# Head norms on token lanes and a band mask added by TensorE, in a two-block transformer kernel

## The reference, cut to what matters

```
def rms_norm_2(x, g):                      # over the 64 of one head
    y = xf * rsqrt(mean(xf * xf, axis=-1) + EPS)
    return y * g

# kind C: keys of the tokens (masked to |q - k| <= 128), context keys, and a sink
s_loc = where(abs(qpos - kpos) <= 128, (q @ k.T) * 64 ** -0.5, -inf)
s_ctx = (q @ k_ctx.T) * 64 ** -0.5
p = softmax(concat([s_loc, s_ctx, sink]))

# kind D
yd = global_attention(apply_rope(rms_norm_2(d_q, qn_g)), apply_rope(rms_norm_2(d_k, kn_g)), d_v,
                      rms_norm_2(cd_k, kn_g), cd_v)
```

## Time and profile before

| what | value |
|---|---|
| median of 3 runs | 2424.68 us (2417.89 to 2424.94) |
| the profiled execution's own time | 2422.05 us |
| its span in the trace | 2420.2 us |
| PE busy | 2194.9 us (91%) |
| DVE, ACT, POOL busy | 752.2, 634.4, 739.4 us |
| layer 0's mixer | from about 1040 to 1223 us of the span |
| layer 1's mixer | from about 1782 to 1920 us of the span |

### The profile page before, as it was taken

One profiled execution on the slowest core, in us unless ns is written; L12 is line 12 of the kernel. 1 busy time (PEld: TensorE's weight loads), 2 busy tenths in 40 slices (PEclk: granted clock), 3 DMA queues, 4 the chain that ended last, 5 costly groups with the idle time before them and its releaser, 6 DMA issues.

```text
span 2420.2 us, 32871 instructions
## 1 busy us (share of the span) xinstructions
PE 2194.9 (91%) x13382; PEld 1354.8 (56%) x13382; DVE 752.2 (31%) x1440; ACT 634.4 (26%) x925; POOL 739.4 (31%) x624
## 2 busy tenths in 40 slices
PE   7998999999799999999999999999889996888886
PEld 7876789878687898865543333333257642222221
DVE  4864220122622212377523222222147420010101
ACT  3544333434544334212512000010022420000001
POOL 7665367897283777710300000000000200000000
PEclk9999999999899999999999999999999998999997
DMA  9433759755157697441215899999962369999997
GB/s 299 140 118 126 261 199 317 244 179 178 36 182 254 208 324 241 143 177 39 86 53 209 341 427 429 429 429 428 424 232 78 134 277 423 427 428 429 429 428 307
DMA packets 151381, 635.98 MB, mean 263 GB/s; under 512 B 7816, under 2 KB 14216, under 8 KB 120920
## 3 DMA queue, kind: packets, MB, share of 16 engines
q1 hardware_dynamic: 148224, 623.78, 66.4%
q0 software_dynamic: 2608, 9.25, 1.3%
q10 hardware_dynamic: 424, 1.22, 0.2%
HBM read 633.17 MB, written 1.05 MB: 262 GB/s over the span
## 4 chain that ended last, share of the span: by engine, by line
PE 65%; DMA 20%; DVE 7%; ACT 3%; POOL 3%; issue 2%; SPq 1%; DVEq 0%; ACTq 0%; POOLq 0%
PE bank L1375 14%; PE bank L624 9%; PE bank L626 9%; PE bank L625 9%; DMA ring<-in_w_gate 9%; DMA ring<-in_w_up 8%; PE bank L1188 4%; PE bank L1333 3%; DMA ring<-in_w_down 3%; PE bank L847 2%; PE bank L1197 2%; PE bank L970 2%; POOL ring_r L1639 2%; PE bank L824 1%; PE bank L1205 1%
## 5 line engine op out<-in xcount | busy, mean ns | idle before, releaser
L1375 PE MATMUL bank<-ring,arena 128*32 128x512 f32 x4424 | 657.4, 630 | 120.6 <-DMA ring<-in_w_gate 53.9
L1639 POOL TENSOR_TENSOR ring_r<-ring,ring_r 128x512 fp32r<-128x512 f32 (+1 forms) x468 | 575.2, 1274 | 294.4 <-ACT ring_r L1734 265.6
L1375 PEld LDWEIGHTS bank<-ring,arena 128*32 128x32 f32 x4424 | 192.7, 115 | 560.3 <-issue 536.6
L624 PE MATMUL bank<-ring_r 128*128 128x256 f32 (+1 forms) x1504 | 463.4, 308 | 14.2 <-POOL ring_r L1639 8.6
L626 PE MATMUL bank<-xT_r,ring_r 128*128 128x256 f32 x1248 | 354.9, 284 | 0.0
L625 PE MATMUL bank<-ring_r 128*128 128x256 f32 x1104 | 312.9, 283 | 0.0
L624 PEld LDWEIGHTS bank<-ring_r 128*128 128x128 f32 x1504 | 289.8, 193 | 37.4 <-issue 18.0
L1734 ACT ACTIVATE ring_r<-ring 128x2048 fp32r<-128x2048 f32 (+1 forms) x119 | 216.7, 1827 | 289.2 <-DMA ring<-in_ffn_w_gu 141.2
L626 PEld LDWEIGHTS bank<-xT_r,ring_r 128*128 128x128 f32 x1248 | 240.1, 192 | 0.0
L625 PEld LDWEIGHTS bank<-ring_r 128*128 128x128 f32 x1104 | 211.6, 192 | 0.7 <-issue 0.5
L1668 POOL TENSOR_TENSOR arena<-const 128x1024 f32<-128x1024 f32 x6 | 12.0, 2003 | 594.8 <-DVEq L2288 525.5
(11 more groups left out here) (356 smaller groups left out, 2720.3 us busy)
## 6 DMA issues: line engine op xcount, KB each, us to landing
ring<-in_w_gate SPq DMA_DIRECT2D x52, 2048.0 KB, 17.2
ring<-in_w_up SPq DMA_DIRECT2D x52, 2048.0 KB, 17.3
ring<-in_w_down SPq DMA_DIRECT2D x40, 2048.0 KB, 18.1
ring<-in_ada_w SPq DMA_DIRECT2D x41, 1024.0 KB, 7.5
ring<-in_w_down SPq DMA_DIRECT2D x41, 1024.0 KB, 18.2
ring<-in_ffn_w_gu SPq DMA_DIRECT2D x35, 1024.0 KB, 5.6
ring<-in_w_up SPq DMA_DIRECT2D x18, 1024.0 KB, 8.7
ring<-in_w_gate SPq DMA_DIRECT2D x17, 1024.0 KB, 5.0
```

Source lines behind the costliest of these rows:

```text
L624: pe.matmul(dst, w_hi, v_hi, start=first, stop=False)
L1375: mm = pe.matmul(dst[nb][CAP * b:CAP * b + CAP, :], src[:, c, CAP * b:CAP * b + CAP], rooms[b % G], start=bi_first, stop=bi_last)
L1639: pool.tensor_tensor(lo[:, c], whole[:, c], hi_of(u)[:, c, 0:n], ALU.subtract).then_inc(*signal("w_lo", (u, c)))
```

## The change

The squares' sums of kind D come out with tokens on the partitions: per tile of 128 tokens the squares are the stationary operand and two columns of `blk64` (one for each head) move, so that a chunk's sums are 128x8 (128x4 for layer 1's queries). Mean, root and reciprocal run on these. Then `spread_norms` brings the inverses back: for each tile and head one product has the token lane's inverse, repeated 64 times by a stride of 0, as the stationary operand and the identity as the moving one, and writes 64 partitions of 128 columns. DVE multiplies with this from the bank. `dq0`, `dq1` are spread between `square_sums2` of `dk0` and the rotations of `cq0`, `cq1`; `dk0` after chunk `ab0`. The banks are 6, 7 and 5; banks 6 and 7 are also those of the rotations of `cq0` and `cq1`.

The band mask becomes a product of the identity with the mask's 256 columns, added to the first key block's scores in the bank, between the products of key block 0 and 1. A masked unit then takes DVE's and ACT's path of a unit without one.

```diff
-        qvar = area(1024, 2, 2 * SEQ)
+        qvar = area(1024, 3, 2 * 4)
@@ unit, block2_units
-  keys=256 * len(tok), size=1024, bias=con("winmask")...
+  keys=256 * len(tok), size=1024, mask=con("winmask")...
@@
+        NORM_AT = dict(dq0=0, dq1=1, dk0=2)
+        SPREAD_BANK = dict(dq0=6, dq1=7, dk0=5)
@@ scores (PE)
                             for c in range(nk):
+                                masked = u["mask"] is not None and kb == 0
                                 mm = pe.matmul(b[:, at:at + 256], u["q"][c][:, t * P:t * P + P], u["k"][kb][c],
-                                               start=(c == 0), stop=(c == nk - 1))
+                                               start=(c == 0), stop=(c == nk - 1 and not masked))
+                            if masked:
+                                mm = pe.matmul(b[:, at:at + 256], ident, u["mask"][:, t, :], start=False, stop=True)
@@ square_sums2 (PE)
-                        pe.matmul(b[:, 0:n], con("blk64"), sq[:, i, 0:n], start=True, stop=True).then_inc(...)
+                        for t in range(n // P):
+                            mm = pe.matmul(b[:, 2 * t:2 * t + 2], sq[:, i, P * t:P * t + P], con("blk64")[:, ::HD], start=True, stop=True)
+                        mm.then_inc(*filled_now(("qss", layer, name)))
+                def spread_norms(names):
+                    for name in names:
+                        n = n_tok if name[1] == "q" else 2 * SEQ
+                        pe.wait_ge(*after("ssq", ("root", layer, name)))
+                        b = open_bank(("rn", layer, name), SPREAD_BANK[name])
+                        for t in range(n // P):
+                            for h in range(2):
+                                one_head = qvar[:, NORM_AT[name], 2 * t + h:2 * t + h + 1].to_broadcast([P, HD])
+                                mm = pe.matmul(b[HD * h:HD * h + HD, P * t:P * t + P], one_head, ident, start=True, stop=True)
+                        mm.then_inc(*filled_now(("rn", layer, name)))
@@ order (PE)
                             square_sums2(("dk0",))
+                            spread_norms(("dq0", "dq1"))
                             rotations(("cq0", "cq1"))
@@
                         chunk("ab0", wb, 0)
+                        spread_norms(("dk0",))
                         rotations(("ck0", "dq0", "dq1"))
@@ roots (ACT)
+                        v = qvar[:, NORM_AT[name], 0:2 * (n_tok if name[1] == "q" else 2 * SEQ) // P]
-                        act.activation(qvar[:, i, 0:n], qvar[:, i, 0:n], ACT.Sqrt).then_inc(...)
+                        act.activation(v, v, ACT.Sqrt).then_inc(...)
@@ norms (DVE), n = 2 * tokens / 128 in the sums and reciprocals
+                    for name in names:
+                        dve.wait_ge(*after("rstd", ("qk", layer, name)))
+                        link(dve.reciprocal(r, r))
+                        done("ssq", ("root", layer, name))
+                    for name in names:
+                        dve.wait_ge(*full(("rn", layer, name)))
-                        link(dve.scalar_tensor_tensor(v, v, col(...), qvar[:, i, 0:n], ALU.mult, ALU.mult))
+                        link(dve.scalar_tensor_tensor(v, v, col(...), bank_of(key)[:, 0:n], ALU.mult, ALU.mult))
+                        drop(key)
```

More of the change, by code:

```diff
@@ L503, in build, with unit @@
         block = ctx.enter_context(nc.Block())
-        def unit(stage, i, q, k, scale, v, y, keys=256, bias=None, sink_at=None, size=512, parts=None):
-            return dict(deep=4 if size == 1024 and i not in (2, 3) else 2, key=(stage, i), n=i, q=q, k=k, scale=scale, v=v, y=y, keys=keys, bias=bias, sink=sink_at, size=size, parts=parts)
+        def unit(stage, i, q, k, scale, v, y, keys=256, bias=None, sink_at=None, size=512, parts=None, mask=None):
+            return dict(deep=4 if size == 1024 and i not in (2, 3) else 2, key=(stage, i), n=i, q=q, k=k, scale=scale, v=v, y=y, keys=keys, bias=bias, sink=sink_at, size=size, parts=parts, mask=mask)
         def half(t, c, j, n0=0, n=SEQ):
@@ L547, in block2_units @@
                                        [(y_hi[64 * (h % 2):64 * (h % 2) + 64, 2 * kind + h // 2, SEQ * s:SEQ * s + SEQ], 64 * (h % 2))],
-                                       keys=256 * len(tok), size=1024, bias=con("winmask").rearrange("p (t k) -> p t k", t=2)
+                                       keys=256 * len(tok), size=1024, mask=con("winmask").rearrange("p (t k) -> p t k", t=2)
                                        if (kind, s) == (0, 0) else None, sink_at=sink[:, layer, h:h + 1] if kind == 0 else None))
@@ L1215, in square_sums2 @@
                         b = open_bank(("qss", layer, name), 4 + i)
-                        pe.matmul(b[:, 0:n], con("blk64"), sq[:, i, 0:n], start=True, stop=True).then_inc(*filled_now(("qss", layer, name)))
+                        for t in range(n // P):
[11 more added lines that the diff above has]
+                        mm.then_inc(*filled_now(("rn", layer, name)))
                 def rotations(names):
@@ L2152, in roots @@
                     for name in names:
-                        n, i = n_tok if name[1] == "q" else 2 * SEQ, int(name[2])
+                        v = qvar[:, NORM_AT[name], 0:2 * (n_tok if name[1] == "q" else 2 * SEQ) // P]
                         act.wait_ge(*after("ssq", ("qk", layer, name)))
-                        act.activation(qvar[:, i, 0:n], qvar[:, i, 0:n], ACT.Sqrt).then_inc(*signal("rstd", ("qk", layer, name)))
+                        act.activation(v, v, ACT.Sqrt).then_inc(*signal("rstd", ("qk", layer, name)))
                 if layer:
@@ L2794, in _ @@
                 for names, others in ((("dq0", "dq1"), ("cq0", "cq1")), (("dk0",), ("ck0",))):
-                    for i, name in enumerate(names):
-                        n = n_tok if name[1] == "q" else 2 * SEQ
+                    for name in names:
+                        n = 2 * (n_tok if name[1] == "q" else 2 * SEQ) // P
                         key = ("qss", layer, name)
                         dve.wait_ge(*full(key))
-                        link(dve.tensor_scalar(qvar[:, i, 0:n], bank_of(key)[:, 0:n], 1.0 / HD, EPS, ALU.mult, ALU.add))
+                        link(dve.tensor_scalar(qvar[:, NORM_AT[name], 0:n], bank_of(key)[:, 0:n], 1.0 / HD, EPS, ALU.mult, ALU.add))
                         drop(key)
                         done("ssq", ("qk", layer, name))
-                    for i, name in enumerate(names):
+                    for name in names:
+                        r = qvar[:, NORM_AT[name], 0:2 * (n_tok if name[1] == "q" else 2 * SEQ) // P]
+                        dve.wait_ge(*after("rstd", ("qk", layer, name)))
+                        link(dve.reciprocal(r, r))
+                        done("ssq", ("root", layer, name))
+                    for name in names:
                         n = n_tok if name[1] == "q" else 2 * SEQ
-                        dve.wait_ge(*after("rstd", ("qk", layer, name)))
-                        link(dve.reciprocal(qvar[:, i, 0:n], qvar[:, i, 0:n]))
+                        key = ("rn", layer, name)
+                        dve.wait_ge(*full(key))
                         v = qk[:, QK_AT[name], 0:n]
-                        link(dve.scalar_tensor_tensor(v, v, col("qn" if name[1] == "q" else "kn", layer), qvar[:, i, 0:n], ALU.mult, ALU.mult))
+                        link(dve.scalar_tensor_tensor(v, v, col("qn" if name[1] == "q" else "kn", layer), bank_of(key)[:, 0:n], ALU.mult, ALU.mult))
+                        drop(key)
                         done("rms", ("qk", layer, name))
```

## The result

The changed kernel took 2429.61 us (median; 2427.39 to 2434.65 over the seven executions compared) against 2420.07 for the kernel before in the same comparison (eight executions, 2414.82 to 2424.94): ratio 1.0037, 95% interval 1.0024 to 1.0051. One further execution of the changed kernel, 2544.08 us at a mean clock of 0.866, is a slow one and stands outside these numbers. So the change costs about 9.5 us, 0.4%. The profiled execution of the changed kernel took 2427.39 us, with a span of 2425.6.

The account below looks back on a forecast made before the run. PE was taken to set layer 0's pace, while in layer 1 it waits for DVE and ACT. Layer 0's +10.7 us (spreads, mask products, shape changes, new wait) and layer 1's 0 gave 2434 us, range 2424 to 2440.

Parts of the forecast that it names:

- What decides: Layer 0 up to `ah1`: PE alone sets the pace, so added PE work is paid in full, DVE relief worth nothing.
- Squares' sums: PE's sums of squares in the norms: 0 of change, bounds -0.1 and +0.1 us for each of six chunks.
- Mean, root, reciprocal: Norms on 128x8: 0.3 us each, hidden behind PE in layer 0, shortening the chain before `dk0`'s rotation in layer 1.
- Spreads: PE products bringing inverses back: 3.4 us in layer 0, 2.2 in layer 1, plus 0.7 us of shape changes per layer.
- the alternating halves of the earlier trace: Lower bound for one spread instruction on PE: the two halves run beside each other, 0.055 us at 128 columns.
- The full-width row: Upper bound for one spread instruction on PE: a full-width product with 128 moving columns, 0.114 us.
- The new wait: PE waits for DVE's multiplication before the rotation of `cq1`: 0.4 us in layer 0, bounds 0.2 and 1.0.
- Mask products and shape changes: PE's masked units, each layer: 3.4 us for the products, 3.0 us for changes of the array's shape around them.
- the +4.7 of the rival: Free shape changes in an unbroken PE group: 3.0 us less in each layer, +4.7 us, 2428; chance 23%.
- Layer 1: Second mixer: 2.4 us gained up to the scores, 2.3 lost from there to `ah1`; +0.1 gained, taken as 0.
- To the end: Output projection and experts after both mixers: both layers' differences pass to the end in full, net +10.7 us.
- the rival at 6%: Layer 0's experts absorb its 10.7 us delay, leaving layer 1's gain: -2 us, 2422; chance 6%.

Follow-up runs that it names:

- e2: Only the band mask's half of the change, norms as in the kernel before: 2429.29 us against 2422.99 for the kernel before, ratio 1.0024.
- e8: The changed kernel with spreads ordered as all tiles of head 0, then head 1: 2428.73 us against 2424.48 for the kernel before, one execution.
- e3: The changed kernel with the mask's products put into the banks before the scores: 2422.56 us against 2422.99 for the kernel before, ratio 0.9987.
- e7: The kernel of e4 run again: 2424.41 us against 2424.48 for the kernel before, ratio 0.9996.
- e4: The whole change in layer 1 alone, layer 0 as in the kernel before: 2430.80 us against 2422.99 for the kernel before, ratio 1.0022.

## Why the prediction was right

**What decides.** Right: in layer 0 every added instruction was paid, and the relief of DVE was worth nothing (e2: all of 6.13 us). Of the 10.5 us that the stages lost, 10.2 stand ahead of layer 0's `ah1`.

**Squares' sums.** Taken at 0: 16 instructions from 1098.10 to 1099.91 are 1.81 us, the four of before 1.82 (1098.56 - 1096.74); `dk0`'s eight take 0.88 (1114.88 - 1114.00) against 0.86. So 0 is right. With 2 moving columns one instruction takes 0.113 us (1.81 / 16), as much as one with 128.

**Mean, root, reciprocal.** Taken at 0.3 us each. The mean at 1120.96 and the end of the reciprocal at 1121.75 in layer 0 give 0.8 us for the three, hidden as said.

**Spreads.** Taken at 0.07 us an instruction plus 0.36 us for each pair of shape changes. One instruction took 0.054 us (see e8), 2.6 us for 48, where 3.4 were predicted: exactly the bound that the alternating halves of the earlier trace rows had given. The tile's shape set the pace, the loading of weights added nothing to be seen, and I should have taken that bound. The full-width row was far off. The Trainium skill, "TensorE: Matmul & The Clock Gate", Part 3, has a load overlap a running product only where their row groups differ; by the prediction's estimate from it the loads would have added about 2.5 us in layer 0, and the trace disagrees, since the 48 took 2.6 us in all.

**The new wait.** 0.4 us predicted in front of the rotation of `cq1`; the row shows 0.32. But that isn't all it costs: there are 0.12 us more in front of the rotation of `cq0`, and the two rotations take 1.50 us (1118.48 - 1116.98) where they took 0.87 (1114.30 - 1113.43): behind a wait the two instructions of one rotation start 0.29 us apart instead of 0.22, and the next group starts later too. That makes 0.75 us, inside the bounds of 0.2 to 1.0. All of the norms' half in layer 0 is 4.05 against 4.5; 2.6 and 0.75 taken off, 0.7 are left for the changes of shape, as predicted. So two terms were mis-sized against each other, the spreads by 0.8 us too much and the wait by 0.35 too little, and it is luck that the sum came out within 0.5.

**Mask products and shape changes.** 3.4 + 3.0 us predicted, less 0.2 for the wait in front of `ah0`, so 6.2; 6.13 measured in layer 0's stage, of which e3 gives 3.04 to the changes. Two units' scores took 6.94 us, forecast 6.7 to 7.1. This term made the difference between "slower" and "no change to be told": without it the sum would have been the +4.7 of the rival.

**Layer 1.** Gain of 2.4 us to the scores predicted, 2.20 measured; PE's wait there 1.0 predicted, 1.09 measured; from there to `ah1` 2.3 lost predicted, 2.55 measured. Net +0.1 gained predicted, 0.35 lost. Waits and low clock that the change removed paid for its products but for these 0.35 us. How much the low clock behind a wait takes is not fixed: after the same 3.16 us the chunk took 6.10 us in the kernel before and 4.57 in e2, and e2's stage came out 1.15 us shorter, so some of layer 1's balance lies with the execution or the code around it.

**To the end.** 10.5 us of stages, 9.5 in the medians: the experts did not absorb layer 0's delay, which the rival at 6% had them do (634.9 us before, 631.8 and 634.4 after). That nothing comes back at all is not shown: behind layer 1's `ah1` the prediction had put nothing, and the two profiles of the changed kernel are over 3 us shorter there (528.4 and 528.7 us against 531.8), nearly all of it in the routing. If that is the change's doing, the forecast left out a term of -3.2 us. The forecast was +10.7 and 2434 us. It measured +9.5, and 2429.6 because the kernel before itself came out 4.6 us lower than in its three first runs.

## What to carry to other kernels

Before moving work to an engine, ask of each stage which engine is full there: the same edit lost 10.2 us in layer 0 and nearly nothing in layer 1, and it wanted a switch by layer. When small products of another tile shape are put between others, price the changes of shape (here about 0.18 us each) beside the columns, and place them next to work of their own shape: the same mask products cost half once they stood first. A small difference is best read from stages between two marks in the profiles, which repeat to hundredths for the same kernel here while whole times scatter by 20 us. But the stretches outside the changed ones have to be read too, and in more than one profile of each kernel: here one of them may have given a third of the loss back.

## What the runs showed of the hardware

- A change of the array's tile shape between 128\*128 and 64\*128 costs PE 0.18 to 0.2 us, in the middle of an accumulation and without any semaphore there: 3.04 us for sixteen, 0.19 each (e3).
- Products of 128\*64 with 128 moving columns start every 0.109 us in one half of the array and every 0.054 us where the two halves alternate; ordered by half, the last four instructions of one half and the first four of the other still ran side by side (e8).
- At full width one fp32 instruction took 0.113 us with 2 moving columns (changed kernel) and 0.114 with 128.
- After the same wait of 1.45 us in the same code the clock stayed up in one execution (e7) and dropped to 1.2 GHz for some 16 us under unbroken work of 64\*128 and 128\*128 in another (e4), which cost 8 us.
